# Feed-forward up units made token-major in the wide form, turned by VectorE block transposes and SBUF-to-SBUF transfers

## The chip, the cores and the metric

The kernel runs on one core of one Trainium2 chip. The metric is the device time of one execution in microseconds (us). PE is TensorE, DVE is VectorE, ACT is ScalarE, POOL is GpSimd and SP is SyncE, whose queue issues the loads of the weights.

## The reference

Two transformer blocks run one after the other over 256 tokens of width 2048, in float32. The change touches their feed-forward parts alone:

```
# block one: w_up 2048 x 8192, w_down 8192 x 2048
u2 = rmsnorm(h, g_mlp_pre)
ff = jnp.square(jax.nn.relu(u2 @ w_up)) @ w_down
h = h + rmsnorm(ff, g_mlp_post)

# block two: w_up 2048 x 11264, w_down 5632 x 2048
h = rms_norm(x, ffn_norm_g)
a, g = jnp.split(h @ w_up, 2, axis=-1)
a = causal_dwconv(a, conv_w, conv_b)      # 3 taps along the tokens
x = x + (jax.nn.gelu(a, approximate=False) * g) @ w_down
```

The other parts are attention in several kinds, an mLSTM and gates.

## The kernel before

All matrix products are made from split operands: a float32 value is kept as a high part and a low part, and a product is the sum of three, high by high, high by low and low by high.

**Halves.** Weights arrive in `raw`, a ring of 4 granules of 1 MB that SP loads (L360). A granule is two *halves* of 1024 weight columns by 128 rows. ACT makes the high part of a half (`hi`, L565), DVE the low part (`lo`, L1196), both into `split`, a ring of 4 halves. PE takes them in order. `hi` of half k waits until PE is through with half k-4, `lo` waits for `hi`, and PE waits for `lo` of each half (`lo_done`). In step m of a unit list both engines first split half m+3 and then do what else stands at m (`each_half`, `after(m)`), so that whatever an engine waits for in `after(m)` stands ahead of its later splits.

**Two forms.** In the *feature form* (`blocks`, L2033 and L2035) the weights stay in the array and the tokens stream: four matmuls of 512 columns wide or 256 for each 128 rows by 256 weight columns. The sums come out with features on the partitions, as high product and cross product side by side; ACT copies the one (`cross`, L571), DVE adds the other (L1209) and multiplies by the row of token norms (L1211). In the *wide form* (`wide_tile`, L2043 to L2045) a tile of 128 tokens stays and 512 weight columns stream, three matmuls for each 128 rows and 128 tokens. The sums come out with tokens on the partitions. Down units have the wide form, and their staying operand `X2` must have the hidden features on the partitions, split as well.

**ffn1** runs four times (b). Each time, four up steps i of two 256-column units fill 16 tiles of `X2`, and two down steps of two 512-column units follow. In an up step, units are finished at m = 3 and 7: DVE takes relu and square (L1587), ACT makes the high part of the hidden tile (L853), DVE its low part (L1589), and the down units wait for these tiles in pairs (`hid_ready`).

**ffn2** runs twice with 8 up steps (16 tiles) and **ffn2b** once with 6 (12 tiles). An up step makes one unit of `a` and one of `g`. At m = 3 DVE brings `a` into the padded tile `a_pad` and makes the three taps (L1929, L1932, L1935), ACT makes Gelu at m = 5 (L1121), and at m = 7 DVE multiplies by `g` (L1942) and splits (L1944, ACT L1125). Down units follow.

The order of the work is written out by hand for every engine; semaphores with counts tie the engines together. GpSimd only issues small transfers on its own queue.

Of the kernel before, what the change touches and what calls it, by code (L numbers as in the profile page):

```python
# [49 lines left out]
def constants():  # L50
# [126 lines left out]
def two_blocks(nc, a, out):  # L177
# [29 lines left out]
    a_pad = E[:, 0:3, :].rearrange("p a b -> p (a b)")[:, 0:2 * (TOK + 2)].rearrange("p (j t) -> p j t", j=2)  # L207
# [8 lines left out]
    t_tok = t[:, :, :, :].rearrange("p a b c -> p (a b c)").rearrange("p (q c) -> p q c", q=2)  # L216
    gate_w = sg[:, 0, :].rearrange("p (k c) -> p k c", k=KT)
# [45 lines left out]
    def vec(name, k):  # L263
# [35 lines left out]
        sem(n) for n in ("qk_squares", "qk_root", "qk_normed", "qk_turned", "q_ready", "k_ready"))  # L299
    out_landed = sem("out_landed")  # L300
# [19 lines left out]
    TWO = plan([full1, full1])  # L320
    OUT1 = GATE = plan([wide1, wide1])
# [22 lines left out]
    def squared(k):  # L344

        return 8 * (k - 1)

# [4 lines left out]
    def _(sp):  # L352
# [73 lines left out]

        def ffn1(b):
            def up(i):
                s = At("ffn1", i, 4, 2, outer_turn=b * 8, outer_units=b * 12, outer_cross=b * 8)
                for u in range(2):  # L430
                    unit(s, 2 * u, a["w_up"][0], b * 2048 + i * 512 + u * COL)

            def down(i):
                s = At("ffn1", i, 8, 2, g=16, u=8, outer_turn=b * 8, outer_units=b * 12, outer_cross=b * 8)
                for u in range(2):
                    wide(s, 4 * u, a["w_down"][0], i * (2 * WIDE) + u * WIDE, row0=b * 2048)
            loop(sp, Chain(None), 4, 0, up)
            loop(sp, Chain(None), 2, 0, down)
# [24 lines left out]
        def ffn2(name, b, pairs, rows):  # L463

            turn, units, cross_units = (b * 12, b * 20, b * 16) if name == "ffn2" else (0, 0, 0)
            col0 = b * 2048 if name == "ffn2" else 4096

            def up(i):
                s = At(name, i, 4, 2, outer_turn=turn, outer_units=units, outer_cross=cross_units)
                unit(s, 0, a["w_up_2"][0], col0 + i * COL)  # L470
                unit(s, 2, a["w_up_2"][0], FF2 + col0 + i * COL)

            def down(i):
                s = At(name, i, 8, 2, g=4 * pairs, u=2 * pairs, outer_turn=turn, outer_units=units, outer_cross=cross_units)
                for u in range(2):
                    wide(s, 4 * u, a["w_down_2"][0], i * (2 * WIDE) + u * WIDE, row0=col0)
            loop(sp, Chain(None), pairs, 0, up)
            if name == "ffn2":
                loop(sp, Chain(None), 2, 0, down)
            else:  # L480
                for n in range(4):
                    wide(At(name, g=4 * pairs), 3 * n, a["w_down_2"][0], n * WIDE, row0=col0, rows=rows)
        loop(sp, Chain(None), 2, 0, lambda b: ffn2("ffn2", b, 8, 2048))
        ffn2("ffn2b", 0, 6, 1536)
# [13 lines left out]
    def _(pool):  # L498
# [45 lines left out]
        pool.wait_ge(conv_done, FFT2 // 2)  # L544
# [5 lines left out]
    def _(act):  # L550
# [276 lines left out]

        def ffn1(b):
            first = isinstance(b, int) and b == 0
            outer = dict(outer_turn=b * 8, outer_units=b * 12, outer_cross=b * 8)  # L830

            def up(i):
                s = At("ffn1", i, 4, 2, **outer)

                def after(m):
                    if first and isinstance(i, int):
# [10 lines left out]
                        if m == 5:  # L847
                            row(1, 0, rn[:, 1, :])
                    if m in ((6, 7) if first and isinstance(i, int) else (3, 7)):
                        u = m // 7  # L850
                        k = b * 8 + 2 * i + u
                        act.wait_ge(hid_done, k + 1)
                        A(X2[:, bass.ds(4 * i + 2 * u, 2), 0, :], t[:, (s.u + u) % 2], ACT.Copy).then_inc(hid_hi, 1)  # L853
                each_half(s, TWO, after)

            def last_down(i):
                s = At("ffn1", i, 8, 2, g=16, u=8, **outer)

                def after(m):
                    if m % 8 == 7:  # L860
# [24 lines left out]
            if first:  # L885
                up(0)
            loop(act, steps, 4, 0, up, start=int(first))
            if isinstance(b, int) and b == 3:
                last_down(0)
                end_by_tiles(At("ffn1", 1, 8, 2, g=16, u=8, **outer))  # L890
            else:
                loop(act, steps, 2, 0, plain("ffn1", DOWN, 16, 8, (8, 2), **outer))
# [72 lines left out]
        def gate_steps(m):  # L965
# [11 lines left out]
            if m == 4:  # L977
                row(2, 3, mix_rn)
# [125 lines left out]
        def ffn2(name, b, pairs, k0):  # L1104
# [1436 lines left out]
```

## Time and profile before

| | |
|---|---|
| median of three runs | 2754.02 us (2753.57 to 2754.55) |
| the profiled execution | 2753.58 us, its span 2751.8 us |
| busy PE | 2743.5 us, 100% of the span |
| busy DVE, ACT, POOL | 1710.7 us (62%), 1363.1 us (50%), 19.1 us (1%) |
| weights moved | 510.64 MB on SP's queue |
| granted clock of PE | 1.000 |

The span reaches from the first to the last instruction of the trace. Busy time of PE counts matmuls whose ends are modelled and which overlap, so the length of one matmul isn't what it costs in a stream; a stretch of the trace divided by its halves is.

### The profile page before, as it was taken

How to read it: one execution, taken by the hardware profiler on the slowest of the kernel's cores; microseconds unless marked ns; L12 is line 12 of the kernel's file. 1: busy time of each engine (PE TensorE's matmuls, PEld its weight loads, DVE VectorE, ACT ScalarE, POOL GpSimd, SP SyncE). 2: the span in 40 equal slices, each digit the busy share in tenths (PEclk: the TensorE clock that was granted, in tenths of full speed). 3: DMA queues.
4: the chain of work that ended last, by engine and by line, in shares of the span. 5: the costliest groups of instructions: out<-in, count | busy, mean ns of one | idle time of the engine just before them, and what ended most of it. 6: DMA issues, size and time to landing. Idle time of an engine off the chain costs nothing.

```text
span 2751.8 us, 37694 instructions
## 1 busy us (share of the span) xinstructions
PE 2743.5 (100%) x14078; PEld 2331.2 (85%) x14078; DVE 1710.7 (62%) x2107; ACT 1363.1 (50%) x1810; POOL 19.1 (1%) x34
## 2 busy tenths in 40 slices
PE   9999999999999999999999999999999999999999
PEld 7888888888888888888888888888888888888887
DVE  7666665555755646556576656665776477657655
ACT  6454554446444434444467555654544344444453
POOL 0000000000000000000000000000000000000000
PEclk9999999999999999999999999999999999999999
DMA  8555556565656565565555655555555555556654
GB/s 298 182 170 183 181 173 202 184 192 182 194 198 186 196 192 177 205 188 193 205 181 198 205 169 183 160 169 189 183 187 191 191 188 192 187 181 194 232 183 140
DMA packets 380438, 521.61 MB, mean 190 GB/s; under 512 B 8516, under 2 KB 254736, under 8 KB 379696
## 3 DMA queue, kind: packets, MB, share of 16 engines
q1 hardware_dynamic: 377760, 510.64, 56.4%
q0 software_dynamic: 2576, 9.58, 1.2%
q8 instruction: 68, 1.11, 0.2%
q14 instruction: 34, 0.28, 0.0%
HBM read 515.98 MB, written 4.21 MB: 189 GB/s over the span
## 4 chain that ended last, share of the span: by engine, by line
PE 98%; DVE 1%; ACT 0%; issue 0%; ACTq 0%
PE ps L2033 32%; PE ps L2035 16%; PE ps L2043 16%; PE ps L2045 16%; PE ps L2044 16%; PE pw L2106 1%; PE pw L2181 0%; DVE split L1196 0%; PE pw L2148 0%; PE pw L2122 0%; PE pw L2159 0%; PE pw L2154 0%; PE pw L2147 0%; PE pw L2407 0%; PE pw L2366 0%
## 5 line engine op out<-in xcount | busy, mean ns | idle before, releaser
L1196 DVE TENSOR_TENSOR split<-raw,split 128x1024 fp32r<-128x1024 f32 x960 | 1158.0, 1222 | 764.0 <-ACT split L565 759.8
L565 ACT ACTIVATE split<-raw 128x1024 fp32r<-128x1024 f32 x960 | 1006.2, 1056 | 881.7 <-PE ps L2045 596.5
L2033 PE MATMUL ps<-X,split 128*128 128x512 f32 x3328 | 1047.4, 396 | 0.3 <-DVE split L1196 0.2
L2035 PEld LDWEIGHTS ps<-X,split 128*128 128x128 f32 x3328 | 625.2, 188 | 147.6
L2043 PE MATMUL ps<-split,X 128*128 128x512 f32 x1912 | 749.0, 392 | 0.7 <-DVE X L1239 0.4
L2045 PE MATMUL ps<-split,X 128*128 128x512 f32 x1912 | 744.4, 389 | 0.0
L2044 PE MATMUL ps<-split,X 128*128 128x512 f32 x1912 | 744.1, 389 | 0.0
L2035 PE MATMUL ps<-X,split 128*128 128x256 f32 x3328 | 653.9, 278 | 0.0
L2033 PEld LDWEIGHTS ps<-X,split 128*128 128x128 f32 x3328 | 508.0, 189 | 2.5 <-issue 1.2
L2045 PEld LDWEIGHTS ps<-split,X 128*128 128x128 f32 x1912 | 358.9, 188 | 75.5
L2043 PEld LDWEIGHTS ps<-split,X 128*128 128x128 f32 x1912 | 359.0, 188 | 74.7 <-issue 1.1
L2044 PEld LDWEIGHTS ps<-split,X 128*128 128x128 f32 x1912 | 359.0, 188 | 73.0
L571 ACT ACTIVATE cross<-ps 128x512 f32<-128x512 f32 x120 | 71.8, 599 | 194.1 <-PE ps L2035 194.0
L2033 PE MATMUL ps<-split,X 128*128 128x512 f32 x512 | 162.8, 399 | 0.0
L2035 PEld LDWEIGHTS ps<-split,X 128*128 128x128 f32 x512 | 96.2, 188 | 22.7
L2035 PE MATMUL ps<-split,X 128*128 128x256 f32 x512 | 100.7, 278 | 0.0
L2033 PEld LDWEIGHTS ps<-split,X 128*128 128x128 f32 x512 | 78.2, 189 | 0.6 <-issue 0.4
L1209 DVE TENSOR_TENSOR t<-ps,cross 128x512 f32<-128x512 f32 x58 | 40.1, 691 | 60.5 <-ACT cross L571 60.5
L853 ACT ACTIVATE X<-t 128x512 f32 (+1 forms) x32 | 20.2, 632 | 75.6 <-DVE t L1587 75.6
L1209 DVE TENSOR_TENSOR E<-ps,cross 128x512 f32<-128x512 f32 x45 | 31.1, 691 | 42.6 <-ACT cross L571 41.6
L1589 DVE TENSOR_TENSOR X<-t,X 128x512 f32 (+1 forms) x32 | 22.2, 692 | 32.2 <-ACT X L853 32.2
L1125 ACT ACTIVATE X<-t 128x512 f32 (+1 forms) x22 | 13.9, 631 | 53.2 <-DVE t L1942 53.2
(257 smaller groups left out, 1049.8 us busy)
## 6 DMA issues: line engine op xcount, KB each, us to landing
raw<-in_w_up SPq DMA_DIRECT2D x152, 1024.0 KB, 5.7
raw<-in_w_in SPq DMA_DIRECT2D x134, 1024.0 KB, 5.1
raw<-in_w_down SPq DMA_DIRECT2D x108, 1024.0 KB, 5.1
raw<-in_w_out SPq DMA_DIRECT2D x32, 1024.0 KB, 5.0
raw<-in_w_ple_gate SPq DMA_DIRECT2D x32, 1024.0 KB, 5.0
raw<-in_w_br_moba SPq DMA_DIRECT2D x8, 1024.0 KB, 5.0
raw<-in_w_br_diff SPq DMA_DIRECT2D x8, 1024.0 KB, 5.0
raw<-in_w_ple_proj SPq DMA_DIRECT2D x4, 1024.0 KB, 5.8
```

The costliest lines, as they stand in the source:

```text
L565: A(split[:, k % RING, :, 0, :], raw[:, (k // 2) % RING, HALF * (k % 2):HALF * (k % 2) + HALF, :], ACT.Copy).then_inc(hi_done, 1)
L571: A(cross[:, s], ps[:, 2 * s:2 * s + 2, TOK:512], ACT.Copy).then_inc(cross_done, 1)
L853: A(X2[:, bass.ds(4 * i + 2 * u, 2), 0, :], t[:, (s.u + u) % 2], ACT.Copy).then_inc(hid_hi, 1)
L1196: TT(split[:, k % RING, :, 1, :], raw[:, (k // 2) % RING, HALF * (k % 2):HALF * (k % 2) + HALF, :], split[:, k % RING, :, 0, :], ALU.subtr ...
L1209: steps.step(TT(dst, ps[:, 2 * s:2 * s + 2, 0:TOK], cross[:, s], ALU.add))
L1589: TT(X2[:, bass.ds(4 * i + 2 * u, 2), 1, :], tile, X2[:, bass.ds(4 * i + 2 * u, 2), 0, :], ALU.subtract).then_inc(hid_ready, 1)
L2033: MM(ps[:, 2 * s + j, :], stay[:, 0, j * P:j * P + P], move, start=start, stop=False, skip_group_check=True)
L2035: ins = MM(ps[:, 2 * s + j, 0:TOK], stay[:, 1, j * P:j * P + P], move[:, 0, :], start=False, stop=stop, skip_group_check=True)
L2043: MM(dst, x_hi, w[:, :, 0, :], start=start, stop=False, skip_group_check=True)
L2044: MM(dst, x_hi, w[:, :, 1, :], start=False, stop=False, skip_group_check=True)
L2045: ins = MM(dst, x_lo, w[:, :, 0, :], start=False, stop=stop, skip_group_check=True)
L2106: ins = T(pw[:, 2 * (c % 2) + pair, k * TOK + q * P:k * TOK + q * P + P], rows[:, q, kt * P:kt * P + P], ident)
```

## The change

All up units turn to the wide form with 512 columns, two for each step of 16 halves (`UP`), so that an up step of ffn1 makes eight tiles and one of ffn2 four of `a` and four of `g`. Their sums have tokens on the partitions. They are brought back to features on the partitions in four steps:

1. ACT evacuates the two banks with the token norms as a scale (`keep_tokens`), with relu and then square in ffn1.
2. DVE transposes blocks of 32x32 into `cross` (`turn_blocks`, two instructions of 128x512).
3. GpSimd's queue moves the blocks across partitions (`move_blocks`): for each of 4x4 pairs of partition groups one transfer of 32 partitions x 2 x 128 elements, 16 for a unit, 256 in ffn1 and 352 in ffn2.
4. ACT, or DVE for `g`, waits for the count of `moved` of all 16 (`wait_for_move`) and goes on: high and low part of the hidden tiles in ffn1 (five halves after the unit's end), the copy into `a_pad` at m = 12, the taps at m = 13, Gelu at m = 14, the product with `g` at m = 3 of the next step and the split at m = 4.

The norm rows of these stages and the additions of cross products fall away. SP loads the up weights as 512 columns of 512 rows instead of 256 columns of 1024 rows.

```diff
-    ("ffn1", 4, 32, 12, 4), ("gate1", 2, 8, 2, 2),
+    ("ffn1", 4, 32, 8, 8), ("gate1", 2, 8, 2, 2),
...
-    ("ffn2", 2, 48, 20, 4), ("ffn2b", 1, 36, 16, 4), ("gate2", 2, 8, 2, 2),
+    ("ffn2", 2, 48, 12, 12), ("ffn2b", 1, 36, 10, 10), ("gate2", 2, 8, 2, 2),
...
+    def move_blocks(queue, n, dst):
+        queue.wait_ge(blocks_made, n + 1)
+        for a in range(4):
+            for b in range(4):
+                src = cross_flat[32 * a:32 * a + 32].rearrange("p (q b c) -> p q b c", q=2, b=4)[:, :, b, :]
+                queue.dma_start(dst[32 * b:32 * b + 32].rearrange("p (q a c) -> p q a c", q=2, a=4)[:, :, a, :], src).then_inc(moved, 16)
+    def wait_for_move(eng, n):
+        eng.wait_ge(moved, 256 * (n + 1))
... GpSimd
+        for n in range(FFN2_MOVES):
+            move_blocks(pool, n, t_flat)
...
+        for n in range(FFT2 // 2):
+            move_blocks(pool, FFN2_MOVES + n, g_moved if n % 2 else a_moved)
... ACT
+        def keep_tokens(s, m, u, k, func):
+            act.wait_ge(half_used, s.halves(m) + 1)
+            act.wait_ge(evac_done, s.unit(u))
+            bank = 2 * ((s.u + u) % 2)
+            for q in range(2):
+                ins = A(t_tok[:, q, :], ps[:, bank + q, :], func, scale=norm_col[:, k, q:q + 1])
...
+        def hidden_hi(k, tiles):
+            for pair in range(2):
+                p0 = 2 * pair
+                A(in_groups(X2[:, 4 * k + p0:4 * k + p0 + 2, 0, :]), tiles[:, p0:p0 + 2], ACT.Copy).then_inc(hid_hi, 1)
... ACT, ffn1
+            def finish(k):
+                wait_for_move(act, b * 4 + k)
+                hidden_hi(k, by_features(t_flat))
...
+                    if m == 4 and i:
+                        finish(2 * i - 1)
+                    if m == 12:
+                        finish(2 * i)
... ACT, ffn2
+                    if m == 4 and i:
+                        finish(i - 1)
+                    if m % 8 == 7:
+                        keep_tokens(s, m, m // 8, 7, ACT.Copy)
+                    if m == 12:
+                        wait_for_move(act, FFN2_MOVES + 2 * c)
+                        A(in_groups(a_pad[:, :, 2:TOK + 2]), by_features(a_moved), ACT.Copy).then_inc(padded, 1)
+                    if m == 14:
+                        act.wait_ge(conv_done, c + 1)
+                        for j in range(4):
+                            ins = A(gelu[:, j, :], conv[:, j, :], ACT.Gelu, bias=vec("conv_b_2", 4 * c + j))
... DVE
+        def turn_blocks(n, second):
+            dve.wait_ge(tokens_kept, n + 1)
+            nc.vector.transpose(cross_tok[:, 0, :], by_blocks(t_tok[:, 0, :]))
+            dve.wait_ge(*second)
+            nc.vector.transpose(cross_tok[:, 1, :], by_blocks(t_tok[:, 1, :])).then_inc(blocks_made, 1)
... DVE, ffn2
+            def gate_hidden(i):
+                c = c0 + i
+                wait_for_move(dve, FFN2_MOVES + 2 * c + 1)
+                dve.wait_ge(sig_done, 4 + c + 1)
+                TT(in_groups(conv), by_features(g_moved), in_groups(gelu), ALU.mult).then_inc(hid_done, 1)
...
+                    if m == 3 and i:
+                        gate_hidden(i - 1)
+                    if m == 4 and i:
+                        finish(i - 1)
+                    if m % 8 == 7:
+                        turn_blocks(32 + 2 * c + m // 8, (evac_done, s.unit(m // 8) + 1))
+                    if m == 13:
+                        convolve(c)
... PE
-            loop(pe, Chain(None), pairs, 0, lambda i: each_half(At(name, i, 4, 2, **outer), TWO, x1_is(5)), start=int(first))
+            for i in range(pairs):
+                each_half(At(name, i, 8, 2, **outer), UP, x1_is(5), start_up if c0 + i == 0 else None)
```

DVE's program at the first up step of ffn2, before. `split` rows are the low parts of halves; `E` is the padded tile, `t` first the taps and then the unit of `g`, `sg` the result of Gelu.

```order
L1196 TENSOR_TENSOR split<-raw,split 128x4x256 x2
L1209 TENSOR_TENSOR E<-ps,cross 128x2x256
L1211 TENSOR_TENSOR E<-E,rn 128x2x256
L1929 TENSOR_SCALAR t<-E,cols 128x256 x2
L1932 SCALAR_TENSOR_TENSOR t<-E,cols,t 128x256 x2
L1935 SCALAR_TENSOR_TENSOR t<-E,cols,t 128x256 x2
L1196 TENSOR_TENSOR split<-raw,split 128x4x256 x4
L1209 TENSOR_TENSOR t<-ps,cross 128x512
L1211 TENSOR_TENSOR t<-t,rn 128x512
L1942 TENSOR_TENSOR t<-t,sg 128x512
L1944 TENSOR_TENSOR X<-t,X 128x2x256
```

The same place after the change, starting behind the two transposes of the first `a` unit. `cross` holds the turned blocks, `G` the moved ones, the taps and Gelu's result, each in a part of its own.

```order
L1274 TENSOR_TENSOR split<-raw,split 128x4x256 x6
L2013 TENSOR_SCALAR G<-E,cols 128x256 x4
L2016 SCALAR_TENSOR_TENSOR G<-E,cols,G 128x256 x4
L2019 SCALAR_TENSOR_TENSOR G<-E,cols,G 128x256 x4
L1274 TENSOR_TENSOR split<-raw,split 128x4x256 x2
L1643 STREAM_TRANSPOSE cross<-t 128x512
L1645 STREAM_TRANSPOSE cross<-t 128x512
L1274 TENSOR_TENSOR split<-raw,split 128x4x256 x4
L2001 TENSOR_TENSOR G<-G 128x1024
L1274 TENSOR_TENSOR split<-raw,split 128x4x256
L1653 TENSOR_TENSOR X<-G,X 128x2x256 x2
L1274 TENSOR_TENSOR split<-raw,split 128x4x256 x3
```

One step now holds 16 halves instead of 8. The taps of four tiles stand between two splits in one piece (12 instructions), the product with `g` stands three splits into the next step, ahead of the split of m = 4, and it waits for a move.

ACT's program at the first up step of ffn2, before:

```order
L565 ACTIVATE split<-raw 128x4x256 x3
L571 ACTIVATE cross<-ps 128x512
L599 ACTIVATE rn<-pw 128x256
L565 ACTIVATE split<-raw 128x4x256 x2
L1121 ACT_TABLE_LOAD
L1121 ACTIVATE sg<-t,cols 128x256 x2
L565 ACTIVATE split<-raw 128x4x256 x2
L571 ACTIVATE cross<-ps 128x512
L1125 ACTIVATE X<-t 128x2x256
```

The same place after the change. L866 are the two evacuations of a unit, L1194 is the copy into the padded tile that waits for the move, L1198 is Gelu, L875 are the high parts of the hidden tiles.

```order
L866 ACTIVATE t<-ps,norm_col 128x512 x2
L597 ACTIVATE split<-raw 128x4x256 x5
L1194 ACTIVATE E<-G 128x4x256
L597 ACTIVATE split<-raw 128x4x256 x2
L1198 ACT_TABLE_LOAD
L1198 ACTIVATE G<-G,cols 128x256 x4
L597 ACTIVATE split<-raw 128x4x256
L866 ACTIVATE t<-ps,norm_col 128x512 x2
L597 ACTIVATE split<-raw 128x4x256 x5
L875 ACTIVATE X<-G 128x2x256 x2
L597 ACTIVATE split<-raw 128x4x256 x3
L866 ACTIVATE t<-ps,norm_col 128x512 x2
```

The copy of L1194 stands five splits after the evacuation and has two splits and Gelu behind it; the rows of L875, which wait for the product with `g`, have three splits and the next evacuation behind them.

GpSimd's queue from the first block on, after the change (numbers behind x count transfers in a row):

```order
L531 DMA gain_rows<-in_g_mix_post 128x512 x2
L531 DMA gain_rows<-in_g_mlp_post 128x512 x2
L375 DMA t<-cross 32x2x128 x256
L554 DMA cross<-in_p_t 128x512
L531 DMA gain_rows<-in_g_mlp_post 128x512 x2
L571 DMA G<-gate_rows 128x2048
L375 DMA G<-cross 32x2x128 x352
L578 DMA E<-ple_kept 128x2048 x2
```

The rows of L375 are new; the loads of `in_p_t`, the gain rows and the return of `ple_kept` are now behind them on this queue.

## Rows read from the trace of the kernel before

**Rows 1.** The page: busy us by engine, and the chain that ended last.
```profile
PE 2743.5 (100%) x14078; PEld 2331.2 (85%) x14078; DVE 1710.7 (62%) x2107; ACT 1363.1 (50%) x1810; POOL 19.1 (1%) x34
...
PE 98%; DVE 1%; ACT 0%; issue 0%; ACTq 0%
```

**Rows 2.** Groups of the page, PE matmuls (busy, mean ns, idle before).
```profile
L2033 PE MATMUL ps<-X,split 128*128 128x512 f32 x3328 | 1047.4, 396 | 0.3 <-DVE split L1196 0.2
...
L2043 PE MATMUL ps<-split,X 128*128 128x512 f32 x1912 | 749.0, 392 | 0.7 <-DVE X L1239 0.4
```

**Rows 3.** Windows, five stretches (busy us of each engine, granted clock, DMA share).
```profile
849.09:938.25 89.16, 89.16 (x513) 77.80 (x512) 58.80 (x62) 41.00 (x46) 0.00 (x0) 1.00 0.59 187
938.25:1025.30 87.05, 87.05 (x386) 72.08 (x385) 45.21 (x39) 34.97 (x34) 0.00 (x0) 1.00 0.59 194
2191.88:2370.21 178.33, 178.33 (x1025) 155.60 (x1024) 125.61 (x157) 85.23 (x102) 0.00 (x0) 1.00 0.57 186
2370.21:2457.26 87.05, 87.05 (x386) 72.11 (x385) 45.21 (x39) 34.89 (x34) 0.00 (x0) 1.00 0.59 197
2457.26:2591.01 133.75, 133.75 (x769) 116.70 (x768) 93.85 (x117) 63.69 (x76) 1.05 (x2) 1.00 0.57 188
```

**Rows 4.** Timeline of DVE in an up step of ffn2 (start, length).
```profile
2006.90 0.62 DVE L1929 TENSOR_SCALAR t<-E,cols 128x256 f32<-128x256 f32 x2
2007.67 0.88 DVE L1932 SCALAR_TENSOR_TENSOR t<-E,cols,t 128x256 f32<-128x256 f32 x2
2008.69 0.88 DVE L1935 SCALAR_TENSOR_TENSOR t<-E,cols,t 128x256 f32<-128x256 f32 x2
2009.49 3.49 DVE L1196 TENSOR_TENSOR split<-raw,split 128x1024 fp32r<-128x1024 f32 x3
```

**Rows 5.** Timeline of ACT in the same stretch (Gelu, a copy, three splits).
```profile
2009.73 0.92 ACT L1121 ACTIVATE sg<-t,cols 128x256 f32<-128x256 f32 x2 [1.17 <-DVE t L1935]
...
2018.94 0.63 ACT L1125 ACTIVATE X<-t 128x512 f32 x1 [2.48 <-DVE t L1942]
2019.48 3.01 ACT L565 ACTIVATE split<-raw 128x1024 fp32r<-128x1024 f32 x3
```

**Rows 6.** Groups by line of GpSimd's transfers (busy us, mean ns of one).
```profile
L531 POOL DMA_DIRECT2D ple_kept<-E x4 | 2.9, 723 | 41.5 <-ACT E L813 41.5
...
L503 POOL DMA_DIRECT2D gain_rows<-in_g_mlp_post x4 | 2.2, 539 | 87.7 <-DVE G L1298 45.2 <-DVE G L1541 42.5
```

**Rows 7.** Timeline of GpSimd, transfers issued one behind another.
```profile
572.20 3.46 POOL L515 DMA_DIRECT2D sg<-in_w_in  x3 [153.16 <-DVE G L1506]
575.64 0.54 POOL L518 DMA_DIRECT2D small<-in_mlstm_gate_bias  x1
576.17 0.53 POOL L518 DMA_DIRECT2D small<-in_fox_f_bias  x1
```

**Rows 8.** DMA issues by line from GpSimd (KB each, median us to landing).
```profile
ple_kept<-E POOLq DMA_DIRECT2D x4, 512.0 KB, 3.5
...
gain_rows<-in_g_ple_post POOLq DMA_DIRECT2D x4, 256.0 KB, 4.8
...
cross<-in_p_t POOLq DMA_DIRECT2D x1, 256.0 KB, 3.0
...
gate_rows<-E POOLq DMA_DIRECT2D x1, 8.0 KB, 3.8
gate_rows<-E POOLq DMA_DIRECT2D x1, 4.0 KB, 1.8
```

**Rows 9.** Groups by line of DVE and ACT, durations of single operations.
```profile
L1589 DVE TENSOR_TENSOR X<-t,X 128x512 f32 (+1 forms) x32 | 22.2, 692 | 32.2 <-ACT X L853 32.2
...
L1359 DVE STREAM_SHUFFLE t<-t 32x1024 f32<-32x1024 f32 x8 | 10.7, 1338 | 0.0
...
L910 ACT ACTIVATE t<-ps,norm_col 128x512 f32<-128x512 f32 x14 | 8.9, 684 | 6.4 <-PE ps L2045 6.4
...
L1298 DVE TENSOR_TENSOR G<-G,gain_rows 128x1024 f32<-128x1024 f32 x6 | 7.3, 1218 | 0.0
```

More of the change, by code:

```diff
@@ L425, in _, with wide_at @@
         proj("proj1", a["w_ple_proj"][0])
+        def wide_at(at, w, col0, row0):
+            wide(at, 0, w, col0, row0)
         def ffn1(b):
[L428 to L438, printed above, removed]
+            for u in range(8):
+                s = At("ffn1", g=4 * u, u=u, outer_turn=b * 8, outer_units=b * 8)
+                if u < 4:
+                    wide_at(s, a["w_up"][0], b * 2048 + u * WIDE, 0)
+                else:
+                    wide_at(s, a["w_down"][0], (u - 4) * WIDE, b * 2048)
         loop(sp, Chain(None), 4, 0, ffn1)
@@ L461, in _, with ffn2 @@
         square("out2", a["w_out_2"][0])
[L463 to L477, printed above, removed]
+        def ffn2(name, b, pairs, c0):
+            outer = dict(outer_turn=b * 12, outer_units=b * 12)
+            col0 = c0 * WIDE
+            for u in range(2 * pairs):
+                wide_at(At(name, g=4 * u, u=u, **outer), a["w_up_2"][0], u % 2 * FF2 + col0 + u // 2 * WIDE, 0)
+            w = a["w_down_2"][0]
             if name == "ffn2":
-                loop(sp, Chain(None), 2, 0, down)
+                for n in range(4):
+                    wide_at(At(name, g=8 * pairs + 4 * n, u=2 * pairs + n, **outer), w, n * WIDE, col0)
             else:
+                s = At(name, g=8 * pairs, u=2 * pairs)
                 for n in range(4):
-                    wide(At(name, g=4 * pairs), 3 * n, a["w_down_2"][0], n * WIDE, row0=col0, rows=rows)
-        loop(sp, Chain(None), 2, 0, lambda b: ffn2("ffn2", b, 8, 2048))
-        ffn2("ffn2b", 0, 6, 1536)
+                    wide(s, 3 * n, w, n * WIDE, col0, 1536)
+        ffn2("ffn2", 0, 4, 0)
+        ffn2("ffn2", 1, 4, 4)
+        ffn2("ffn2b", 0, 3, 8)
         square("gate2", a["w_ple_gate_2"][0])
@@ L1144, in _ @@
-        ffn2("ffn2", 0, 8, 0)
-        ffn2("ffn2", 1, 8, 8)
-        ffn2("ffn2b", 0, 6, 16)
+                down(0)
+                down(1)
+            else:
+                last_down(At(name, g=8 * pairs, u=2 * pairs))
+        ffn2("ffn2", 0, 4, 0)
+        ffn2("ffn2", 1, 4, 4)
+        ffn2("ffn2b", 0, 3, 8)
         def last_gate(s):
@@ L1954, in ffn2, with last_down, after @@
+            def last_down(s):
+                def after(m):
+                    finish_last(m)
+                    if m > 5 and m % 6 == 4:
+                        gained_lo(6, m // 6 - 1, "ple_norm_g_2")
+                    if m % 6 == 5:
+                        add_h(s, m, m // 6, m // 6)
+                each_half(s, DOWN3, after)
+            for i in range(pairs):
+                up(i)
             if name == "ffn2":
-                loop(dve, steps, 2, 0, down)
-            else:
-                last_down(At(name, g=4 * pairs, u=2 * pairs))
@@ L1959, in last_down @@
-        def last_down(s):
-            def after(m):
-                if m > 5 and m % 6 == 4:
-                    gained_lo(6, m // 6 - 1, "ple_norm_g_2")
-                if m % 6 == 5:
-                    add_h(s, m, m // 6, m // 6)
-            each_half(s, DOWN3, after)
-        ffn2("ffn2", 0, 8, 0)
-        ffn2("ffn2", 1, 8, 8)
-        ffn2("ffn2b", 0, 6, 16)
+                down(0)
+                down(1)
+            else:
+                last_down(At(name, g=8 * pairs, u=2 * pairs))
@@ L1971, in gated_tile @@
+        ffn2("ffn2", 0, 4, 0)
+        ffn2("ffn2", 1, 4, 4)
+        ffn2("ffn2b", 0, 3, 8)
         def gated_tile(sig, q, c0, c1):
@@ L2479, in _, with ffn2 @@
         out2(1)
[L2481 to L2483 removed]
+        def ffn2(name, b, pairs, c0):
+            outer = dict(outer_turn=b * 12, outer_units=b * 12)
             def start_up(m):
```

301 lines of the change are left out of this document (155 added, 146 removed).

## The prediction

> **What bounds the kernel now.** I read the head of the page first: PE is busy for 2743.5 of 2751.8 us, and it holds 98% of the chain that ended last [rows 1]. The groups by line say the same: the large matmul groups wait 0.3 and 0.7 us in all [rows 2]. So the time is the sum of what TensorE has to stream, and work on DVE, ACT or GpSimd counts only where it makes PE wait.
>
> Then I cut the trace at the places where the form of the matmuls changes [rows 3]. Of its five stretches the first, third and fifth are up units in the feature form, the second and fourth down units in the wide form. A half (1024 weight columns of 128 rows, split once by ACT and once by DVE) takes 89.16/32 = 2.786, 178.33/64 = 2.786 and 133.75/48 = 2.786 us in the feature form, and 87.05/32 = 2.720 us in the wide one, twice. The granted clock is 1.00 in all of them. Both forms stream 6144 columns for a half (8x512 + 8x256, or 12x512), so what the wide form saves is 4 of 16 instructions, 0.0655 us a half.
>
> **What the change gives on PE.** 128 halves of ffn1 and 176 of ffn2 and ffn2b turn wide: 304 x 0.0655 = 19.9 us. Two norm rows (a matmul of 128x256 each, and what starts around it) go: about 0.7 us. Together -20.6 us. The profiled execution took 2753.58 us and the median is 2754.02, so the sum is made against 2753.6; a measurement tells about 0.2% (5.5 us) from no change.
>
> **What it adds.** The hidden units now come out with tokens on the partitions and must be turned before the down units. For each of 38 up units of 512 columns (16 + 22): two evacuations on ACT, two block transposes on DVE, 16 transfers of 32 partitions x 2 x 512 B on GpSimd's queue, and then a wait for all 16 that stands in ACT's program (in DVE's too, for the gate half). Behind this wait are queued the hi splits on ACT and the lo splits on DVE, and PE waits for each of those within four halves. Busy time is no problem. ACT and DVE have room: they are busy 85 and 126 of 178 us in the third stretch [rows 3]. What matters is one chain in ffn2, whose links I time thus:
>
> - GpSimd: one issue is c, the last transfer lands L after its issue, the move takes M = 15c + L.
> - The nearest rows for c: 0.54 us for a transfer of one run a partition (128 runs) and 0.72 for 128 partitions x 2 runs [rows 6], 0.54 and 0.53 for 4 and 8 runs and 3.46/3 = 1.15 for 128 x 16 runs, one behind another [rows 7]. By number of runs (64) the new ones are near 0.54; by shape (partitions x 2 runs on both sides) they are nearest to 0.72. From 4 to 128 the number of runs costs nothing, and doubling it from 128 to 256 costs 0.18, which I read as the price of the second dimension. I take c = 0.70 and keep 0.54 and 0.72 as ends.
> - The nearest rows for L: 1.8 and 3.8 us for 4 and 8 KB, 3.0 and 4.8 for 256 KB from memory, 3.5 for 512 KB [rows 8]. 32 KB in 64 pieces over the same engines as the weights: I take 2.2, ends 1.8 and 3.0. M = 10.5 + 2.2 = 12.7 us (ends 9.9 and 13.9).
> - The Trainium skill (DMA: Bandwidth & Descriptors, Anatomy of one DMA) gives 2.0 us plus bytes over 436 GB/s for a transfer from this queue, an estimate of 2.1 us for 32 KB. No row here is of this kind; by it M would be 12.6 and the sum 2 us lower.
> - ACT: copy of 128x1024 into the padded tile 1.06; one hi split behind another (3.01-1.06)/2 = 1.0; four Gelu 0.92 + 2x0.41 = 1.75 [rows 5]; an evacuation 0.68, its next one some 0.62 behind [rows 9].
> - DVE: lo split 1.13 behind another, 1.2 alone; the convolution over four tiles from the rows for two (0.77+0.54, 1.02+0.80, 0.88+0.80) = 4.8 [rows 4]; a product of 128x1024 1.2; a subtraction of 128x512 0.65. No block transpose stands in the trace: a product of 128x512 takes 0.69, a shuffle of 1024 takes 1.34 [rows 9], so 0.75 each, ends 0.69 and 1.34.
>
> *Leg one*, from the blocks of the convolved unit to those of the gate unit: M + 1.06 (pad) + 1.0 (hi, m = 13) + 1.15 (lo) + 4.8 (convolution) + 1.75 (Gelu) + 1.0 (hi, m = 15) + 1.2 (lo) + 1.5 (transposes) = M + 13.5. *Leg two*, back to the next pair's first blocks: M + 1.2 (gate) + 1.15 (lo, m = 4) + 1.3 (two subtractions) + 3.4 (three lo) + 1.5 = M + 8.6. The circle is 2M + 22.1 us; PE needs 16 x 2.72 = 43.5 for the same pair. It closes without a stall only for M below 10.7. With M = 12.7 it is 47.5: 4.0 us are lost for each pair that follows another, 3 + 3 + 2 = 8 times, 32.0 us.
>
> *The last pair of a group* has no up unit to hide behind. Its convolved unit's blocks are made some 3.3 us after that unit's end, so its gate unit's at 3.3 + 12.7 + 13.5 = 29.5, which is 7.7 after its own end (a unit lasts 21.8). Then come M, the gate 1.2, lo 1.15 and one subtraction 0.65: 23.4 us. The down unit of ffn2 asks for those tiles at its seventh half (6 x 2.72 = 16.3 us), that of ffn2b, with 12 tiles, at its fifth (10.9): 7.1 us twice and 12.5 once, 26.7 us.
>
> *ffn1* has one move a unit and no convolution. The blocks are ready 1.3 (evacuations) + 1.15 (squares) + 0.8 + 0.1 = 3.5 us after the unit's end, the hidden tiles 12.7 + 0.6 + 0.65 + 0.2 later, 17.7. Inside the up units the next split is wanted only at 21.8 us; in the first down unit the tiles are wanted at 16.3: 1.4 us four times, 5.6.
>
> Sum: 2753.6 - 20.6 + 32.0 + 26.7 + 5.6 = 2797.3; I say 2797 us, slower by 1.6%. At nothing I cost: the loops over ffn1 and ffn2 partly written out (hidden, PE's queue is never short of work now); the loads of the up weights as 4x512 for 8x256 (SP issues as many, and ACT never waits for them); rows of moved data on the DMA engines (512 KB a unit beside 4 MB of weights, at a DMA share of 0.57 to 0.59 [rows 3]); if that cover is gone it shows in L, each 1 us of which is 2 us a pair.
>
> **Rivals.**
> *Faster: an issue costs 0.54.* For it: 8 and 128 runs cost the same [rows 6, 7], and 64 lies between. With L = 2.0, M is 10.1 and the circle 42.3, inside PE's 43.5. The blocks of the last gate unit are made 2.3 + 10.1 + 13.5 - 21.8 = 4.1 us after its end, its tiles at 4.1 + 10.1 + 3.0 = 17.2: 0.9 us late twice, 6.3 in ffn2b, and ffn1 loses nothing: 2753.6 - 20.6 + 8.1 = 2741 us. Against it: the row of the same shape. The sign turns at M = 11.1 or so (c = 0.59 with L = 2.2): there the stalls equal the 20.6 us gained. From 10.8 to 11.4 no change can be told. Chance 0.32, and 0.08 for between.
> *Much slower: issues one behind another don't keep their single price.* No more than six stand back to back in this trace [rows 7], never sixteen. If each takes 1.0 us, M is 17.2 and the circle 56.5: 13 us a pair for 8 pairs, the ends 16.1 twice and 21.5, ffn1 some 15 in each of its four blocks: 2753.6 - 20.6 + 104 + 54 + 60, some 2950 us. Against it: the gain rows cost 0.54 each while DVE is busy for 62% of the time [rows 1, 6]. The Trainium skill (SBUF — State Buffer, Who interferes with whom) has a rule of this kind: descriptors of GpSimd's queue can't be written while a two-port VectorE instruction holds the shared port. The page counts tensor_scalar among those that can be in that mode, and the convolution starts with four of them. By that rule an issue beside them would be late by what they last. No run here shows it yet. Chance 0.12.
> *Slower, my forecast:* M between 11.4 and 14, chance 0.48. With c = 0.725 and L = 3.0, M is 13.9, the circle 49.9, 6.4 a pair (51), the ends 34 and ffn1 10: 2828. Transposes at 1.34 each would add 2.4 us a circle, which carries this to 2850.
> *That the change does nothing* is no case: the form of 304 halves changes, and their price is a row.
>
> **Numbers.** Faster 0.32, within 0.2% 0.08, slower 0.60. The range goes from 2738 (M below 10) to 2850, which leaves out most of the third case. The forecast's own range is 2760 to 2850.
>
> **What the changed profile would show.** PE's up stretches at 2.72 us a half outside the stalls: right or wrong for the 20 us. GpSimd's transfers at 0.70 (mine) or 0.54 (rival) each. Stalls of PE in every ffn2 pair at the last half of its first up unit (the lo split of m = 4, behind the gate product that waits for the move), and in the down units at the seventh half, ffn2b's at the fifth. In ffn1 none in the up units. If PE stalls at the half after the convolution, leg one alone is too long. I am wrong if c is under 0.6, if the transposes take twice what I say, or if the transfers queue behind the weights and L grows past 3.

## The result, and the profile after

The median after is 2802.61 us (2801.67 to 2808.9, five runs), the median before, from five runs beside them, 2753.96 us. The ratio is 1.0182 (95% interval 1.0171 to 1.0193): slower by 1.8%, where 2797 us had been forecast.

The head of the page after, with its chain. It answers to [rows 1], where PE was busy for 100% and held 98% of the chain.

```profile
PE 2741.9 (98%) x12858; PEld 2282.6 (81%) x12858; DVE 1624.0 (58%) x1984; ACT 1387.5 (50%) x1851; POOL 342.5 (12%) x642
...
PE 79%; POOL 7%; DVE 7%; DMA 4%; ACT 2%; issue 1%; ACTq 0%; DVEq 0%
```

A fifth of the chain now leads through other engines: GpSimd's issues, transfers on their way, DVE's and ACT's work between them. DVE is even less busy than before. No engine became the bound; a circle of waits did.

Windows of the trace after (columns as in [rows 3]):

```profile
849.08:936.12 87.04, 87.04 (x386) 72.07 (x384) 47.29 (x46) 42.99 (x50) 25.50 (x48) 1.00 0.65 207
1995.41:2028.07 32.66, 32.66 (x145) 26.98 (x144) 22.54 (x30) 17.13 (x21) 12.71 (x24) 1.00 0.66 215
1995.41:2063.60 68.19, 65.54 (x289) 53.93 (x288) 40.64 (x53) 31.60 (x37) 25.52 (x48) 1.00 0.67 217
2085.20:2089.60 4.40, 4.40 (x13) 3.48 (x14) 4.40 (x5) 2.73 (x3) 0.00 (x0) 0.61 0.75 242
2141.09:2206.37 65.28, 65.28 (x289) 54.05 (x288) 32.81 (x27) 25.45 (x24) 0.00 (x0) 1.00 0.56 186
```

The first row is 32 halves of up units in ffn1: 2.720 us a half, against 2.786 in [rows 3]. The second is twelve halves of an up step in ffn2: 2.72 too. So what the change gives is there in full. The third row is 24 halves and holds 2.65 us in which PE did nothing. The fourth is a single half behind a stall: PE is busy throughout and takes 4.40 us for it, at a granted clock of 0.61. The last is down units: nothing lost.

By stages of the trace: ffn1 went from 708.73 to 709.4 us, ffn2 from 532.1 to 558.34, ffn2b from 201.75 to 222.78, each other stage kept its length, and the first matmul came 1.0 us later.

Waits of the trace after (us in total, times, longest):

```profile
DVE G L2001 <- DMA G<-cross: 86.8, 11, 9.2
...
ACT X L875 <- DMA t<-cross: 69.6, 16, 8.0
...
ACT E L1194 <- DMA G<-cross: 40.5, 11, 6.2
```

These are the three places at which ACT and DVE wait for a move, with their counts: 11 products with `g`, 16 units of ffn1, 11 copies into the padded tile.

Groups by line of GpSimd's transfers, and the DMA issues with their median time to landing:

```profile
L375 POOL DMA_DIRECT2D G<-cross x352 | 187.2, 540 | 928.2 <-DVE cross L1645 715.0 <-issue 213.1
L375 POOL DMA_DIRECT2D t<-cross x256 | 136.1, 540 | 502.9 <-DVE cross L1645 397.8 <-issue 104.9
```

```profile
G<-cross POOLq DMA_DIRECT2D x352, 32.0 KB, 4.6
...
t<-cross POOLq DMA_DIRECT2D x256, 32.0 KB, 4.7
```

One issue costs 0.540 us, the price of the rival that was faster; the landing takes 4.6 us, more than any case had allowed. 15 x 0.54 + 4.6 = 12.7 us, which is the forecast's M to the tenth, out of two errors that cancel. For the last transfer of a move alone, the one that counts, the landing took 3.6 to 5.7 us, 4.5 in the median. Counted from the end of the transposes to the last landing, a move took 11.8 to 13.9 us in 35 cases (with some 0.3 us ahead of the first issue), and 16.0 to 16.6 in three.

One round of the circle, in the timelines of GpSimd, then of DVE:

```profile
1978.50 8.52 POOL L375 DMA_DIRECT2D G<-cross  x16 [17.27 <-DVE cross L1645]
```

```profile
1990.06 1.23 DVE L2001 TENSOR_TENSOR G<-G 128x1024 f32<-128x1024 f32 x1 [7.34 <-DMA G<-cross]
1991.20 1.22 DVE L1274 TENSOR_TENSOR split<-raw,split 128x1024 fp32r<-128x1024 f32 x1
1992.34 1.28 DVE L1653 TENSOR_TENSOR X<-G,X 128x512 fp32r<-128x512 f32 x2
1993.54 3.49 DVE L1274 TENSOR_TENSOR split<-raw,split 128x1024 fp32r<-128x1024 f32 x3
1996.95 0.70 DVE L1643 STREAM_TRANSPOSE cross<-t 128x512 f32<-128x512 f32 x1
1997.57 0.67 DVE L1645 STREAM_TRANSPOSE cross<-t 128x512 f32<-128x512 f32 x1
```

GpSimd issues for 8.52 us, the last transfer lands at 1990.06, 3.0 us after the issues' end, and DVE, which had waited for 7.34 us with all later splits behind it, works without a gap until the next pair's blocks are made at 1998.2.

### The profile page after: what moved, and what is told of

It reads as the page before. It is cut to its first block, busy times and chain, and to the rows that moved or that the text cites. A ratio compares the mean times of both kernels' runs of the same rounds, so it can differ in the third digit from the quotient of the medians.

```text
span 2800.8 us, 33601 instructions
## 1 busy us (share of the span) xinstructions
PE 2741.9 (98%) x12858; PEld 2282.6 (81%) x12858; DVE 1624.0 (58%) x1984; ACT 1387.5 (50%) x1851; POOL 342.5 (12%) x642
## 4 chain that ended last, share of the span: by engine, by line
PE 79%; POOL 7%; DVE 7%; DMA 4%; ACT 2%; issue 1%; ACTq 0%; DVEq 0%
PE ps L2151 20%; PE ps L2153 20%; PE ps L2152 20%; PE ps L2141 11%; PE ps L2143 6%; POOL G L375 5%; DMA G<-cross 3%; DVE split L1274 2%; POOL t L375 1%; ACT split L597 1%; DMA t<-cross 1%; DVE G L2016 1%; DVE G L2019 1%; PE pw L2214 1%; DVE cross L1645 1%
## 5 line engine op out<-in xcount | busy, mean ns | idle before, releaser
L2151 PE MATMUL ps<-split,X 128*128 128x512 f32 x3128 | 1230.3, 393 | 51.6 <-DVE X L1653 27.4
L2153 PE MATMUL ps<-split,X 128*128 128x512 f32 x3128 | 1222.3, 391 | 0.0
L2152 PE MATMUL ps<-split,X 128*128 128x512 f32 x3128 | 1221.5, 391 | 0.0
L2151 PEld LDWEIGHTS ps<-split,X 128*128 128x128 f32 x3128 | 590.1, 189 | 184.4 <-issue 32.5
L2153 PEld LDWEIGHTS ps<-split,X 128*128 128x128 f32 x3128 | 589.6, 188 | 123.9
L2152 PEld LDWEIGHTS ps<-split,X 128*128 128x128 f32 x3128 | 590.7, 189 | 120.7
L375 POOL DMA_DIRECT2D G<-cross x352 | 187.2, 540 | 928.2 <-DVE cross L1645 715.0
L2141 PE MATMUL ps<-X,split 128*128 128x512 f32 x896 | 283.0, 397 | 0.0
L2143 PEld LDWEIGHTS ps<-X,split 128*128 128x128 f32 x896 | 168.3, 188 | 39.7
L375 POOL DMA_DIRECT2D t<-cross x256 | 136.1, 540 | 502.9 <-DVE cross L1645 397.8
L2143 PE MATMUL ps<-X,split 128*128 128x256 f32 x896 | 176.1, 278 | 0.0
L2141 PE MATMUL ps<-split,X 128*128 128x512 f32 x512 | 162.8, 399 | 0.0
L2141 PEld LDWEIGHTS ps<-X,split 128*128 128x128 f32 x896 | 137.1, 189 | 1.1 <-issue 0.5
L2143 PEld LDWEIGHTS ps<-split,X 128*128 128x128 f32 x512 | 96.2, 188 | 22.7
L2141 PEld LDWEIGHTS ps<-split,X 128*128 128x128 f32 x512 | 78.2, 189 | 0.6 <-issue 0.4
L866 ACT ACTIVATE t<-ps,norm_col 128x512 f32<-128x512 f32 x76 | 47.9, 681 | 35.4 <-PE ps L2153 32.3
L2001 DVE TENSOR_TENSOR G<-G 128x1024 f32<-128x1024 f32 x11 | 13.5, 1225 | 86.8 <-DMA G<-cross 86.8
L603 ACT ACTIVATE cross<-ps 128x512 f32<-128x512 f32 x44 | 26.3, 597 | 66.5 <-PE ps L2143 66.3
L1653 DVE TENSOR_TENSOR X<-t,X 128x512 fp32r<-128x512 f32 x32 | 20.7, 688 | 60.1 <-ACT X L875 60.1
```

The lines of the kernel that those rows point to most:

```text
L375: queue.dma_start(dst[32 * b:32 * b + 32].rearrange("p (q a c) -> p q a c", q=2, a=4)[:, :, a, :], src).then_inc(moved, 16)
L866: ins = A(t_tok[:, q, :], ps[:, bank + q, :], func, scale=norm_col[:, k, q:q + 1])
L2141: MM(ps[:, 2 * s + j, :], stay[:, 0, j * P:j * P + P], move, start=start, stop=False, skip_group_check=True)
L2143: ins = MM(ps[:, 2 * s + j, 0:TOK], stay[:, 1, j * P:j * P + P], move[:, 0, :], start=False, stop=stop, skip_group_check=True)
L2151: MM(dst, x_hi, w[:, :, 0, :], start=start, stop=False, skip_group_check=True)
L2152: MM(dst, x_hi, w[:, :, 1, :], start=False, stop=False, skip_group_check=True)
```

## Experiments

All are changes to the kernel after, and each ratio is to the kernel before, measured on the same chip. For each trace M is the time from the end of a unit's transposes to the last landing, and the period that of a pair of up units, from the blocks of one `a` unit to those of the next. PE alone needs 43.52 us for a pair.

### One transfer for sixteen

```diff
-                queue.dma_start(dst[...][:, :, a, :], src).then_inc(moved, 16)
+        queue.dma_start(dst, cross_flat).then_inc(moved, 16)
```

Both loops around it go, and the waits count one transfer.

> The 16 transfers of a move become one of 128 partitions x 1024 elements, the same 512 KB; it leaves out the crossing of partitions. Theory A (the circle of two moves and the work between them is longer than PE's pair of units, 2M + 22.1 against 43.5 us): M falls from 12.4 to about 5, no stall is left, the clock stays at 1.00 and the time is 2754 - 20.6, some 2734 us. Rival B (the added work on ACT and DVE, or the moved bytes, cost the time, not the length of the move): within 10 us of the changed kernel's 2803.

Measured: 2739.48 us, ratio 0.9947 (0.9924 to 0.9969). M was 3.3 to 3.8, but for two moves (4.3 and 5.3), all periods 43.5; ffn1 took 699.9 us, ffn2 523.2. The only stall left is in the first down unit of ffn2b, 3.2 us, with 1.7 behind it at a lowered clock. With a short move the change gives its 20 us less that end, so the added work on ACT and DVE and the moved bytes cost nothing by themselves.

### Eight transfers of 64 partitions

```diff
-        for a in range(4):
+        for r in range(2):
             for b in range(4):
-                src = cross_flat[32 * a:32 * a + 32]...
+                src, to = (x[64 * r:64 * r + 64]... for x in (cross_flat, dst))
```

> Eight transfers of 64 partitions x 2 x 128 for a move, the same bytes; the crossing of partitions is left out. Theory A: M = 7 x 0.54 + 4.5 = 8.3 us, under the 10.7 at which the circle closes; only the last pair of ffn2b is late by a few us: 2736 us. Rival B: 2800. Halfway, at 2765 or so, if each issue's place in the row isn't what the landing depends on.

Measured: 2752.73 us, ratio 0.9995 (0.9984 to 1.0007): no change that could be told. The periods are 43.5, as expected. But M was 8.9 to 11.6 us and not 8.3 (12.8 and 13.6 in two moves, in the midst of which GpSimd paused for 3.0 us), and the time 17 us above what I expected: an issue costs 0.598 us, and a landing takes 5.1 to 5.2. The ends pay for that (2.2, 3.7 and 7.7 us, each followed by one half at a lowered clock, 1.5 to 1.8 us more), 19 us together. M lies inside the circle and still the whole gain is gone, by the ends alone.

### Twenty transfers

```diff
                 queue.dma_start(dst[...][:, :, a, :], src).then_inc(moved, 16)
+                if a == 3:
+                    queue.dma_start(rn[32 * b:32 * b + 32, :, 0:128], src).then_inc(moved, 16)
```

> Four transfers more for each move, into a tile that nothing reads then; the waits count 20. Theory A: M grows by 4 x 0.54 = 2.2 us, each of 11 pairs loses two of these (47 us) and ffn1's four blocks one each at their end (9), and some ring of the clock's drops: 2860 us. Rival C (the last landing is set by the gaps between weight loads, not by the row of issues): steps of a load, so either nothing or some 3 us for each move, 2803 or 2880.

Measured: 2876.94 us, ratio 1.0445 (1.0415 to 1.0476). Leg one was M + 12.92 us in every pair, as in the kernel after; the longer periods (48.2 to 55.1 us) came for the most part from M, 13.1 to 16.2 us, and 17.7 to 19.2 in five moves. In the median M grew by 1.7 us (14.5 for 12.8) and not by 2.2: the last transfer landed 3.5 us after its issue instead of 4.5. Even so the time was 17 us above what I expected: in the midst of those five moves GpSimd paused for 5.5 to 6.8 us, leg two was longer by 0.6 to 1.8 us in six of the eight pairs that follow another, and TensorE ran for 92 us at the lower clock.

### Quarter-size loads of the up weights

```diff
-                    wide_at(s, a["w_up"][0], b * 2048 + u * WIDE, 0)
+                    for q in range(4):
+                        load(s, q, a["w_up"][0][q * 512:q * 512 + 128, bass.ds(b * 2048 + u * WIDE, WIDE)])
```

The same in ffn2; three quarters of the up weights aren't loaded. PE, ACT, DVE and GpSimd do the same work.

> The loads of up weights bring 128 rows of each 512 (a quarter of the bytes); the rest of the tile keeps what it had, so part of the weights is left out. Theory A with landings late because transfers wait behind a weight load of 3 us on the same engines: a transfer's landing falls from 4.6 to about 2 us after its issue, M from 12.4 to some 10, and the time to about 2745 us. Rival D (the queue's own completion takes 4.6 us): landings stay at 4.6 and the time at 2803.

Measured: 2770.48 us, ratio 1.006 (1.0037 to 1.0083). Its DMA issues:

```profile
G<-cross POOLq DMA_DIRECT2D x352, 32.0 KB, 2.2
...
t<-cross POOLq DMA_DIRECT2D x256, 32.0 KB, 2.8
```

With the same number of issues at the same 0.540 us, the landing fell from 4.6 to 2.2 us, and M to 10.0 in 20 moves. The loads of down units kept their size, and the 14 moves that met them took 12.2 to 13.2 us. So half of L in the kernel after is time behind the weights. The time was 25 us above what I expected, since the expectation had left these moves out: the eight pairs that follow another lost 2.4 us in all instead of 29.9, but the ends of the three groups still lost some 28 us.

### Middle tap left out

```diff
-                for j in range(4):
-                    steps.step(STT(conv[:, j, :], a_pad[:, j, 1:TOK + 1], tap(1, j), conv[:, j, :], ALU.mult, ALU.add))
-                settled()
```

> The four DVE instructions of the middle tap are left out (1.8 us of the convolution). Theory A (the circle of moves and the links between them): each second is worth as much in this link as in a move, so leg one falls from M + 12.9 to M + 11.1, the pairs lose some 1.8 us less 8 times and the three group ends as well: 2803 - 20 = 2783 us, a few less if the clock drops fewer times. Rival B (only the waits for the moves at fixed places cost): 2800.

Measured: 2783.2 us, ratio 1.0104 (1.0084 to 1.0124). Leg one fell from M + 12.92 to M + 11.22. 1.7 us less of DVE's work in a leg is worth 19 us in the whole, though DVE is busy for 58% only: work counts in this circle by its length, wherever it runs.

### Product with `g` and the splits behind it two halves later

```diff
-                    if m == 3 and i:
+                    if m == 5 and i:
                         gate_hidden(i - 1)
-                    if m == 4 and i:
+                    if m == 6 and i:
                         finish(i - 1)
```

The same for ACT's `finish`.

> In ffn2's up steps the product with g stands at m = 5 and the split of the hidden tiles at m = 6, instead of 3 and 4; all transfers stay on GpSimd's queue. Theory A: leg two loses the three lo splits that were queued behind the wait, the circle falls from 2M + 21.1 to about 2M + 17, 42 us with M = 12.4, under PE's 43.5. What stays: the ends of the groups (5 us twice, 10.5 once), ffn1's 1.4 four times, some clock: 2765 us. Rival B: no change, 2803, or more since the hidden tiles come later.

Measured: 2789.78 us, ratio 1.0128 (1.0111 to 1.0145). Leg two fell from M + 8.21 to M + 5.94, but the `g` moves themselves rose to about 13.8 us in most pairs, and the periods fell only to 44.8 to 46.1 (48.6 and 49.1 behind two moves that started late). PE now stalls behind the first half of the next step, with nothing left at the old place. The direction was right, the size a third of what I expected (13 us for 38): the wait only went to the neighbouring step, and the ends, which this doesn't touch, kept their stalls (5.8, 5.0 and 11.7 us). Its first stall of that kind, from PE's timeline:

```profile
2017.30 0.47 PE L2151 MATMUL ps<-split,X 128*128 128x512 f32 x1 [1.00 <-DVE split L1274]
```

### Half of the transfers on SyncE's queue, and all of them

```diff
-    def move_blocks(queue, n, dst):
+    def move_blocks(queue, n, dst, groups=(0, 1)):
...
-        for a in range(4):
+        for a in groups:
...
+                if q == 0 and move:
+                    move_blocks(sp, *move, groups=(2, 3))
```

SyncE issues its part behind the first load of the unit after next; it counts on a semaphore of its own. In the other kernel GpSimd has none of them and SyncE all 16.

> SP issues 8 of a move's 16 transfers, behind the first weight load that comes after the unit, with a semaphore of their own; GpSimd issues the other 8. Theory A: M = 7 x 0.54 + 4.5 = 8.3 us, all circles close in PE's time, the ends of the groups lose about 5 us: 2740 us, faster than before by 0.5%. Rival E (the transfers hold up SP's weight loads, or land behind them in the same queue): PE waits for loads, 2760 us or more.

> All 16 transfers on SP's queue, GpSimd none. SP's price of an issue stands in no row. Theory A: if it is under 0.2 us, M is some 6 us and the time 2737 us, as with one transfer; if it is as dear as GpSimd's, M stays over 12 and the time at 2800. Rival E (weight loads held up behind them): stalls of ACT on raw, over 2760.

Measured: half on SyncE 2744.14 us, ratio 0.9963 (0.9949 to 0.9977); all on SyncE 2774.98 us, ratio 1.0077 (1.006 to 1.0094). The DMA issues of the first:

```profile
G<-cross SPq DMA_DIRECT2D x176, 32.0 KB, 1.9
G<-cross POOLq DMA_DIRECT2D x176, 32.0 KB, 1.8
```

And SyncE's timeline in the second:

```profile
1986.90 0.37 SPq L393 DMA_DIRECT2D raw<-in_w_up  x1
1989.25 10.64 SPq L375 DMA_DIRECT2D G<-cross  x16
1999.93 1.69 SPq L393 DMA_DIRECT2D raw<-in_w_up  x3
```

An issue on SyncE costs 10.64/16 = 0.665 us in this row (0.64 to 0.71 from one issue to the next over all its moves), more than on GpSimd. What falls is the landing, to 1.9 us on both queues, also for GpSimd's transfers: while SyncE issues the move it issues no weight load, so none stands in the way. With all 16, M is 11.5 to 12.7, and both legs stayed as they were, 12.93 and 8.21 behind M. There the weights were held up, as rival E says: ACT waited for loads of `w_up` and `w_down` twelve times, 17.5 us together; but since the legs kept their length, the pairs lost nothing by it. With half, ACT didn't wait for these loads, the two queues issue beside each other, M is 6.4 in most moves and not 8.3 (the expectation had left the landing at 4.5), 13.0 in one that GpSimd started 3.4 us late, and the periods are 43.5 to 43.6. Only ffn2b's end stalls (8.1 us, and 1.9 with a lowered clock).

### GpSimd's last loads behind the last move

In the kernel with half on SyncE the last move took 11.9 us instead of 6.4. Its timeline of GpSimd there:

```profile
2575.18 4.26 POOL L375 DMA_DIRECT2D G<-cross  x8 [19.33 <-DVE cross L1650]
2579.43 1.13 POOL L583 DMA_DIRECT2D E<-ple_kept  x2
```

Two loads of 1 MB stand right behind GpSimd's half, while SyncE's half is still being issued (2574.92 to 2580.94).

```diff
         pool.wait_ge(conv_done, FFT2 // 4)
+        pool.wait_ge(moved_by_sp, 128 * 38)
         for q in range(2):
```

> The kernel of the half-on-SyncE run, with one wait more: GpSimd returns `ple_kept` (two loads of 1 MB) only when all moves have landed, not right behind its own half of the last one. In the half-on-SyncE run the last move of ffn2b took 11.9 us from the transposes to its last landing instead of 6.4, and the 1 MB loads were issued 0.0 us behind GpSimd's half, while SyncE's half was still being issued. If these loads delay that move, M of the last move falls from 11.9 to 6.4, and of the 8.1 and 1.9 us that PE stalled in ffn2b's first down unit some 2.6 us are left: about 2737 us, 7.5 below the half-on-SyncE run's 2744.1, ratio to before about 0.994. If the weight loads delay it, nothing changes: 2744.

Measured: 2738.84 us, ratio 0.9945 (0.9931 to 0.9958), the fastest kernel of this study. The time was 5.3 us lower, where 7.5 had been expected. The last move took 7.2 us, and PE lost 3.5, 2.6 and 0.3 us there, part of it at the lower clock, instead of 8.1 and 1.9. PE, and DVE's waits for `g` moves (four in all, the longest 3.4 us), in the trace:

```profile
PE 2726.6 (100%) x12858; PEld 2278.0 (83%) x12858; DVE 1629.9 (60%) x1984; ACT 1393.8 (51%) x1851; POOL 181.0 (7%) x338
...
DVE G L2007 <- DMA G<-cross: 6.1, 4, 3.4
```

So loads of 1 MB delayed the small transfers whether SyncE or GpSimd had issued them.

## Why the prediction came out as it did

**The gain.** 20.6 us had been said, and 2.720 us a half stand in the windows. Right.

**The circle.** The measured links against the forecast's: leg one M + 12.9 for M + 13.5, leg two M + 8.2 for M + 8.6 (M + 8.9 to M + 9.2 in three of the eight pairs), so a circle of 2M + 21.1 for 2M + 22.1, and block transposes of 0.708 and 0.669 us for 0.75. Leg one was 12.91 to 12.93 us in all eleven pairs, and lost 1.7 us with the middle tap. That the two legs and two moves are a closed circle, longer than PE's 43.5 us, is shown by the runs that change one link each. The periods of the eight pairs that follow another were 45.5 to 51.1, against 47.5.

**Two of its own signs of being wrong came true:** c is under 0.6, and L grew past 3. The number was right all the same, by luck.

**c, the price of an issue, was mis-sized:** 0.540 and not 0.70. I took it from the row nearest in shape (128 partitions x 2 runs); that price falls with the partitions, 0.72 for 128 [rows 6], 0.598 for 64, 0.540 for 32 with 2 runs each, down to what the smallest transfers cost too [rows 7].

**L was mis-sized, and outside its ends:** 4.6 us for 2.2 (1.8 to 3.0). With c alone put right the forecast would have been near the rival's 2741 us, with the wrong sign. With L alone put right M would have been 15.1 and the same sum 2753.6 - 20.6 + 70 + 41 + 15, some 2860 us, outside the range. I had named a cause ("the transfers queue behind the weights and L grows past 3") and given it no price. The transfers in the trace in half microseconds show it. Below are packets started and engines busy with them, on the hardware queue (weights) and on the software queue (the move), for a move whose 16 issues began at 1978.50. The busy times of two packets on one engine overlap a little, so the sum can pass 16.

```
start     weights: packets, engines   move: packets, engines
1979.5        0    0.0                32   4.2
1980.0       13    1.8                32   4.0
1980.5       35   13.4                 0   0.0
1981.0       38   13.5                 0   0.0
1981.5       81   16.4                 0   0.0
1982.0      100   16.8                 0   0.0
1982.5       97   16.8                 0   0.0
1983.0      102   16.7                 0   0.0
1983.5       69   10.0                81   7.1
1984.0       48   11.4                47   5.7
1984.5       74   16.6                 2   0.2
1985.0       86   16.4                 3   0.3
1985.5       88   15.8                 9   1.0
1986.0       70   13.9                24   3.0
1986.5       68   14.9                19   2.1
1987.0       62   11.9                52   5.1
1987.5       25    4.3               104  12.4
1988.0        0    0.0                95  13.5
1988.5        0    0.0                12   1.8
```

The two first transfers land in 1.7 and 1.8 us. Then a load of 1 MB keeps 13 to 16 engines busy for some 3 us and nothing of the move gets through until it nears its end; then what has gathered goes at once. The next load does it again, less strictly: for 1.5 us 14 packets of the move start beside 248 of the weights, in the next 1.5 us 95 beside 200, and the rest, 211, goes as the load ends. The last transfer has to outlive whichever load is in flight when it is issued. Three kinds of runs agree: smaller loads bring L to 2.2, no loads meanwhile bring it to 1.9, and loads of 1 MB from GpSimd's queue bring it up again.

The Trainium skill (DMA: Bandwidth & Descriptors, Anatomy of one DMA) gives 2.0 us plus the bytes over 436 GB/s. The first transfers of a move (1.75 us in the median), and those of the runs without loads beside them (1.8 and 1.9), come near its 2.1; the 4.6 of the kernel after doesn't. The same page (Queues, rings and completion order) has each engine go round between its queues packet by packet, with 9 to 17 descriptors in a typical packet and at most 64. What this trace lists as a packet is a piece of 2 KB (or a count for a semaphore), 32 such pieces of a load for each engine. Whether a load's 32 pieces make one packet in the page's sense or several isn't shown, so the rule fits both the first load here and the second, and would not have told me the 4.6.

**M = 12.7** was thus right by two errors of 2.4 us each, and what hangs on it came near. What PE lost, in us, by its excess over 2.720 for a half:

| | forecast | measured | of it at the lower clock, and behind late starts |
|---|---|---|---|
| pairs that follow another, 8 | 32.0 | 29.9 | 6.4, 5.7 |
| ends of three groups | 26.7 | 27.9 | 4.8, 0 |
| ffn1 | 5.6 | 9.0 | 1.7, 1.8 |
| start and small rest | 0 | 2.8 | |

The rest includes 1.5 us at the second half of ffn2b's first down unit. The forecast's sums hold but for small slips (3.35 us called 3.5 in ffn1, 13.8 called 13.9) and one of a microsecond: it lets the blocks of the last pair's first unit be made 3.3 us after that unit's end and its rival 2.3 us. Measured were 2.2, 2.2 and 3.0.

**The places** that had been named were right one by one. PE stalls at the eighth half of the first up unit of each later pair, in ffn1 and ffn2 at the seventh half of the first down unit, in ffn2b at its fifth. Three stalls had not been named, each behind a move that started late (below): 1.8 us inside the up units of ffn1, where none was to be, and 2.8 and 2.9 us at the second half of a later pair in ffn2 and ffn2b. The last two are what the forecast had called the sign that leg one alone is too long; with that late start it was, M + 12.9 = 28.9 and 29.1 us, where PE needs 21.8 for the unit. The largest stall but one, from PE's timeline (the wait in brackets is on the low part of a hidden tile):

```profile
2134.11 0.79 PE L2151 MATMUL ps<-split,X 128*128 128x512 f32 x1 [6.22 <-DVE X L1653]
```

**Not foreseen: the clock.** Before, the granted clock was 1.00 up to PE's last matmul; after, eight stretches of 3.4 to 10.2 us, 37.5 us together, show it at 0.5, that is at 1.2 and not 2.4 GHz, and each begins in a stall of PE of 1.9 us or more (by its excess) or at most 1.2 us behind it (three such stalls, of 1.9, 2.8 and 2.9 us, were followed by none). Where PE worked in them, a half took 4.2 to 4.4 us. That is 13 us, a fifth of what was lost, and the table's stalls proper are the smaller by it: 54 where 64 had been forecast. So the sum was near for the second time by an error that another made good.

**Not foreseen: late starts.** Three moves began 3.39 us after the transposes instead of 0.29, with nothing in the trace that GpSimd waited for. Transposes and first issue of the second of them, from the timelines of DVE and GpSimd:

```profile
2229.69 0.67 DVE L1645 STREAM_TRANSPOSE cross<-t 128x512 f32<-128x512 f32 x1
```

```profile
2233.75 8.51 POOL L375 DMA_DIRECT2D G<-cross  x16 [106.89 <-issue]
```

They stand behind 128, 384 and 512 of the 608 transfers and cost 7.4 us of PE together; behind 256, where GpSimd had waited for 427 us, the first issue was 0.65 us behind the transposes. In the run with 20 transfers a move GpSimd paused for 5.5 to 6.8 us behind 128, 256, 448, 576 and 704 of them, in the run with eight for 3.0 us twice, 128 transfers apart, in the two runs with half on SyncE once, behind 256. With one transfer a move, or none on GpSimd, no pause stands in the trace. So the pauses go by the number of transfers that GpSimd has issued; what GpSimd does then isn't shown by any run.

**The rivals.** The faster one had c right, and with L at 2 the circle closes as it says: in the run with quarter-size loads, where M was 10.0 in most moves, six of the eight pairs that follow another lost nothing, the other two 1.2 us each behind a late start. The one much slower, by issues that don't keep their single price, is refuted: 16 in a row cost 0.54 each, but for the pauses above. Its form with the port shared by DVE's two-port instructions stays open: no issue of a move fell beside the four tensor_scalar of the convolution, since the circle puts them one behind the other.

**Open.** The first matmul came 1.0 us later, 10.89 for 9.92; I didn't look for the cause. The part of the clock is read from the trace, no run was made for it alone.

## What to carry to other kernels

Write a change that adds a round trip as a circle: sum the legs, compare with what the bound engine needs for the same work, and time the ends, where nothing hides the trip, apart; here, with eight transfers, a trip of 8.9 to 11.6 us was free in the circle and still cost 19 us at the ends. A small transfer's landing time must be taken beside the loads that it will meet, not from a row where the engines were idle: here it went from 1.9 to 4.6 us, and giving half of the transfers to the queue that issues the loads took both the issue time and the collision away. When a forecast comes out right, check its terms; two of these were off by 2.4 us each. One put right alone would have turned the sign, the other put right alone would have left the range.

## What the runs showed of the hardware

- Transfers of 32 KB between partitions land in 1.7 to 1.9 us when no load stands in their way, from GpSimd's or SyncE's queue alike, and in 4.6 in the median beside loads of 1 MB. One of 512 KB lands in 3.0 to 3.2 us.
- An issue of 32 partitions x 2 runs costs 0.540 us on GpSimd, of 64 x 2 runs 0.598, the first form on SyncE 0.64 to 0.71.
- GpSimd started a move 3.1 us late at three places, behind 128, 384 and 512 of its 608 transfers.
- In or behind eight of eleven stalls of PE of 1.9 us or more the granted clock went from 1.00 to 0.5, for 3.4 to 10.2 us. The kernel before, without stalls, doesn't show it until PE is through; the slowest kernel has 92 us of it.
- A block transpose of 128x512 in float32 takes 0.69 us on DVE, about as long as a product of that size.
